# An inverse put behind the next row maximum, and a second scale factor of ones, in a two-layer attention trunk

## The reference

```python
for l in range(DEPTH):                       # DEPTH 2, 512 tokens, 1024 channels
    h = rms_norm(x, norm_g[l])
    proj = jnp.einsum('btd,dc->btc', h, w_in[l])
    q_a, kv_a, g_a, z_a, q_b, k_b, v_b, f_b, z_b, merge = jnp.split(proj, split_at, axis=-1)
    y_a = nsa_mixer(q_a, kv_a, g_a, ...) * jax.nn.silu(z_a)
    y_b = fox_mixer(q_b, k_b, v_b, f_b, b_forget[l]) * jax.nn.silu(z_b)
    ...
# NSA: three softmaxes per head, each output times its own gate
    o = g[:, :, 0] * o_cmp + g[:, :, 1] * o_slc + g[:, :, 2] * o_win
# FOX: one softmax per head, no gate on the probabilities
    s = s + Fq[..., None] - F[:, :, None, :]
    p = masked_softmax(s, mask)
    return jnp.einsum('bhqk,bkhd->bqhd', p.astype(v.dtype), v)
```

## Time and profile before

| | us |
|---|---|
| median of 3 runs | 1521.31 |
| lowest, highest | 1521.21, 1521.73 |
| the profiled execution | 1520.49 |
| its span, first to last instruction | 1518.8 |
| PE busy | 1477.1 (97%) |
| DVE busy | 1028.8 (68%) |
| ACT busy | 903.8 (60%) |
| POOL busy | 488.2 (32%) |
| granted TensorE clock, mean | 0.994 of full |

### The profile page before, as it was taken

The page is one execution under the profiler, slowest core; times in us unless marked ns, Lnnn a source line. Parts: engine busy times, 40 slices in busy tenths (PEclk is TensorE's granted clock), DMA queues, the critical chain, the costliest instruction groups (busy, mean ns, idle before and its releaser), DMA issues.

```text
span 1518.8 us, 24823 instructions
## 1 busy us (share of the span) xinstructions
PE 1477.1 (97%) x7605; PEld 1242.0 (82%) x7605; DVE 1028.8 (68%) x2459; ACT 903.8 (60%) x1879; POOL 488.2 (32%) x578
## 2 busy tenths in 40 slices
PE   6999999999999999999998999999999999999997
PEld 5778888888888888888876888888888888888886
DVE  4778788788788874434557778788787787643443
ACT  4667777777777762223446777777777776422233
POOL 1245445455455320000004445355355363000000
PEclk9999999999999999999999999999999999999998
DMA  9222222122122243332452222222222221433332
GB/s 245 70 72 56 57 52 60 47 53 62 49 56 56 57 123 99 89 105 83 126 152 67 60 53 57 55 56 57 56 57 55 55 56 45 149 88 106 89 95 80
DMA packets 221826, 117.84 MB, mean 78 GB/s; under 512 B 17560, under 2 KB 220336, under 8 KB 221232
## 3 DMA queue, kind: packets, MB, share of 16 engines
q1 hardware_dynamic: 219584, 107.66, 26.8%
q0 software_dynamic: 1728, 8.66, 1.5%
q10 hardware_dynamic: 432, 0.54, 0.1%
HBM read 110.41 MB, written 6.42 MB: 77 GB/s over the span
## 4 chain that ended last, share of the span: by engine, by line
PE 84%; DVE 6%; ACT 3%; SPq 2%; issue 2%; DMA 2%; POOL 1%; ACTq 0%; DVEq 0%; POOLq 0%
PE acc L1522 59%; PE o_pair L1600 8%; PE turned L1582 7%; PE scores L1573 4%; PE scores L1574 4%; DMA w_raw<-in_w_in_dram 2%; DVE w_lo L1031 1%; PE misc L1611 1%; SPq L462 1%; DVE c_blk L1310 1%; ACT w_hi L700 1%; SPq L469 1%; DVE yt_lo L1408 1%; PE o_pair L1626 0%; PE turned L1680 0%
## 5 line engine op out<-in xcount | busy, mean ns | idle before, releaser
L1522 PE MATMUL acc<-u_hi,w_hi 128*128 128x512 f32 x1120 | 443.1, 396 | 9.4 <-DVE w_lo L1031 5.8
L1522 PE MATMUL acc<-u_lo,w_hi 128*128 128x512 f32 x1120 | 441.1, 394 | 0.0
L1522 PE MATMUL acc<-u_hi,w_lo 128*128 128x512 f32 x1120 | 440.2, 393 | 0.0
L816 ACT ACTIVATE prob<-prob,row_max 128x128 f32<-128x128 f32 (+3 forms) x384 | 215.3, 561 | 183.4 <-DVE row_max L1197 181.2
L1031 DVE TENSOR_TENSOR w_lo<-w_raw,w_hi 128x1024 fp32r<-128x1024 f32 x188 | 233.8, 1244 | 87.9 <-ACT w_hi L700 85.3
L628 POOL TENSOR_SCALAR prob<-prob,row_inv,gates 128x128 f32<-128x128 f32 (+3 forms) x256 | 173.0, 676 | 331.1 <-DVE row_inv L1204 329.5
L700 ACT ACTIVATE w_hi<-w_raw 128x1024 fp32r<-128x1024 f32 x188 | 198.1, 1054 | 95.4 <-PE acc L1522 85.8
L1522 PEld LDWEIGHTS acc<-u_hi,w_hi 128*128 128x128 f32 x1120 | 211.0, 188 | 51.9 <-DVE w_lo L1031 7.6
L1522 PEld LDWEIGHTS acc<-u_hi,w_lo 128*128 128x128 f32 x1120 | 211.0, 188 | 40.0
L1522 PEld LDWEIGHTS acc<-u_lo,w_hi 128*128 128x128 f32 x1120 | 211.2, 189 | 38.7
L1197 DVE CUSTOM_DVE_ANT_0 prob<-scores,causal 128x128 f32<-128x128 f32 (+3 forms) x384 | 184.9, 481 | 46.4 <-PE scores L1574 37.5
(11 more groups left out here) (195 smaller groups left out, 2235.0 us busy)
## 6 DMA issues: line engine op xcount, KB each, us to landing
w_raw<-in_w_in_dram SPq DMA_DIRECT2D x140, 512.0 KB, 3.8
w_raw<-in_w_proj_nsa_dram SPq DMA_DIRECT2D x16, 512.0 KB, 3.7
w_raw<-in_w_proj_fox_dram SPq DMA_DIRECT2D x16, 512.0 KB, 3.7
w_raw<-in_w_out_dram SPq DMA_DIRECT2D x16, 512.0 KB, 3.7
x_scratch<-xT POOLq DMA_DIRECT2D x2, 2048.0 KB, 9.0
xT<-x_scratch POOLq DMA_DIRECT2D x2, 2048.0 KB, 8.3
x_nat<-in_x_dram SPq DMA_DIRECT2D x4, 512.0 KB, 6.5
c_w<-in_cmp_w_k_dram SPq DMA_DIRECT2D x4, 512.0 KB, 7.8
```

Source lines behind the costliest of these rows:

```text
L816: act.activation(prob[:, ring, 0:width], prob[:, ring, 0:width], ACT.Exp, bias=row_max[:, ring:ring + 1], scale=-1.0, accum_out=row_sum[:, ...
L1522: ins = pe.matmul(acc[par][0:width, :], w[:, par, k, 0:width], rhs, start=(n == 0), stop=(n == 23))
```

## The change

Two edits. In VectorE's stream the maximum of step s now stands ahead of the inverse of step s-1, where it stood behind it. And FOX's scaling gets a second factor per row, the first column of `ones`, so that it has the same form as NSA's.

```diff
@@ scale_step
                 if branch is None:
-                    ins = pool.tensor_scalar(p, p, row_inv[:, ring:ring + 1], None, ALU.mult)
+                    ins = pool.tensor_scalar(p, p, row_inv[:, ring:ring + 1], ones[:, 0:1], ALU.mult, ALU.mult)
@@ VectorE, body of a cycle
+                    if step(0):
+                        max_step(*step(0))
                     if step(LAG_SCALE):
                         invert_step(*step(LAG_SCALE))
-                    if step(0):
-                        max_step(*step(0))
                     if step(LAG_PT):
                         lo_step(*step(LAG_PT))
```

## The result

The changed kernel takes 1528.42 us (median of 5 runs, 1528.10 to 1528.99) where the kernel before takes 1521.21 (5 runs, 1520.81 to 1521.73). The ratio is 1.0048, interval 1.0033 to 1.0063: slower by 7.2 us, and outside of the forecast range. The profiled execution took 1528.11, its span is 1526.4 against 1518.8.

The account below looks back on a forecast made before the run. TensorE was taken as the bound. Per layer +0.20 - 0.70 = -0.50, two layers -1.0, middle cycles 0.0: 1519.5 against the profiled 1520.49, and 1520.3 us as median, range 1519.0 to 1523.5.

Parts of the forecast that it names:

- What bounds the kernel: TensorE, busy throughout the middle cycles; time can be gained only at its six waits in the two layers' last cycles.
- the faster rival: Softmax chain sets the pace: all six TensorE waits go, 3.6 us gained, 1517.7; chance of over 0.2% faster 3%.
- The cost of a late tile: At a transpose on TensorE: a late scaled tile costs its lateness plus 0.11 us; margins under 0.11 begin to cost.
- Part 1, middle cycles, step 7: New order delays the inverse 0.20 us; step 7's margin falls from 0.34 to 0.14, above 0.11, so no cost.
- Part 1, middle cycles, step 13: Inverse later by at most the maximum's 0.53 us; step 13's margin falls from 0.67 to 0.14, so no cost.
- the upper bound of 2.8 us: Middle cycles: delay of 0.35 us costs 1.4 us at step 7, with as much again from steps 11 and 13.
- The second rival: Inverse too late in every middle cycle, at step 7: 1521.7, or 1523.1 with steps 11 and 13; chance 22%, 5% beyond 0.2%.
- Part 2, step 22 of the last cycle: Faster FOX scalings on GpSimd remove TensorE's wait at step 22: -0.70 us per layer, range 0 to -0.70.
- Part 1, last cycle: Step 7's margin is used up, so +0.20 us per layer, 0 to 0.35; the wait for a low part unchanged.
- Part 2, the two-factor form's times: FOX scalings on GpSimd take 0.77, 0.66 and about 0.55 us for 512, 384 and 256 keys.
- The rival that the factor brings no speed: FOX's scalings stay slow for another reason than form: 1522.8 to 1524.2; chance 8%, 2% of it beyond 0.2%.

Follow-up runs that it names:

- late7: qcos_late plus one useless 256-column PSUM copy on VectorE between step 8's maximum and step 7's inverse in the 12 middle cycles; 1523.72 us.
- order_only: Kernel before with only the new order, maximum ahead of inverse; FOX's scaling keeps one factor; 1534.49 us, ratio 1.0083.
- qcos_psum: Changed kernel, but VectorE's cosine product in the cycles reads its first input from a PSUM bank, giving wrong values; 1520.81 us, ratio 0.9996.
- qcos_late: Changed kernel with VectorE's cosine product of the query rotation one slot later, nothing left out; 1520.48 us, ratio 0.9995.
- old_collide: Kernel before, old order and one factor, with the cosine product called ahead of the low part in its slot; 1528.01 us, ratio 1.0039.
- ones_only: Kernel before with only FOX's second factor of ones, old order kept; 1521.43 us, ratio 0.9998.

## Why the prediction was wrong

- **What bounds the kernel**: right. TensorE had no wait in the middle, so nothing could be gained there. The exponential's wait for maxima shrank from 181.2 to 177.3 us and brought nothing; the faster rival was rightly at 3%.
- **The cost of a late tile** (lateness plus 0.11): right, by late7 (0.25 worked out, 0.24 to 0.27 measured) and by step 13 (0.49 late and 0.60 worked out, 0.6 to 0.75 measured). At step 22 of order_only it gives 0.21 where 0.20 to 0.30 is lost.
- **Part 1, middle cycles, step 7: no cost**: right. The delay was forecast at 0.20 and took 0.34 - 0.20 = 0.14 off the margin.
- **Part 1, middle cycles, step 13: no cost**: this is the step that failed. "0.67 - 0.53 = 0.14, no cost" moved the scaling by its delay and let it keep its 0.55. The delay itself was sized safely: 0.27 and not 0.53, so that 0.41 of margin is left without the collision, as qcos_psum shows. What it left out is that a moved instruction gets new neighbours, and that its duration can depend on them. Fourteen scalings came to lie beside the cosine product and took 0.89 us more. Neither the sum nor the upper bound of 2.8 us nor a rival held such a term. It was to be had: the grouped view of the kernel before shows a shape that takes longer than one of twice its size,

```profile
L628 POOL TENSOR_SCALAR prob<-prob,row_inv,gates 128x128 f32<-128x128 f32 x64 | 45.0, 704 | 5.9 <-DVE row_inv L1204 4.3
...
L628 POOL TENSOR_SCALAR prob<-prob,row_inv,gates 128x256 f32<-128x256 f32 x64 | 36.4, 569 | 154.4 <-DVE row_inv L1204 154.4
```

since 14 of the 16 scalings of step 0 take 1.47 us beside VectorE's work, as do step 4's in the first cycle of each layer (1.49), and the others 0.45. FOX's 384-key scalings take 1.25 at step 18 and 1.68 to 1.76 at step 22; the 1.69 stands in the earlier trace rows, and the prediction read it as the form's price.
- **The second rival** (a late inverse in every middle cycle) had the sign and the kind of place: a tile of an NSA step too late for its transpose, twelve times, though it named step 7 ahead of 13, and step 7 cost nothing. Its price was put at 1.4 to 2.8 us and its mechanism, a delay, was another. Its condition, a delay of 0.57, was met in effect by 0.27 of delay and 0.89 of stretch, against the margin of 0.67.
- **Part 2, step 22 of the last cycle: -0.70**: the mechanism was right and the size off. The scaling was taken at 0.66, and took 1.10 beside a product of line 1145 with two SBUF inputs (itself 1.16 long where the kernel before has 0.67 to 0.70: GpSimd's gating ran when it started). The wait shrank to 0.27 us, not to nothing. The timeline there, changed kernel (the GpSimd row groups steps 22 and 23, 1.10 and 0.77 long with hardly a gap):

```profile
543.70 1.16 DVE L1145 SCALAR_TENSOR_TENSOR z_silu<-z_th,z_silu 128x512 f32<-128x512 f32 x1
...
544.29 1.85 POOL L625 TENSOR_SCALAR prob<-prob,row_inv,ones 128x384 f32<-128x384 f32 x2
...
545.12 0.28 PE L1600 MATMUL o_pair<-pt_lo,v_fox 128*128 128x256 f32 x1
...
545.45 0.55 PE L1582 MATMUL turned<-ident,prob 128*128 128x128 f32 x3
```

- **Part 1, last cycle: +0.20 at step 7, the low part's wait unchanged**: wrong in both places. Step 7's wait moved to step 6, whose scaling lies beside the query's low parts (line 1116), and step 13 gained one. Before, the last cycle lost 0.61, 0.59 and 0.70 us at step 7, at the low part and at step 22. After, it loses 0.70, 0.77 and 0.27 at steps 6, 13 and 22: 1.74 against 1.90, where 0.50 less was forecast. Step 6:

```profile
508.69 1.39 DVE L1116 TENSOR_TENSOR q_fox<-qk_raw,q_fox 64x512 fp32r<-64x512 f32 x2 [0.21 <-ACT q_fox L748]
508.75 1.71 POOL L628 TENSOR_SCALAR prob<-prob,row_inv,gates 128x384 f32<-128x384 f32 x1
...
510.51 0.55 PE L1582 MATMUL turned<-ident,prob 128*128 128x128 f32 x3 [0.48 <-POOL prob L628]
```

- **Part 2, the two-factor form's times**: right. FOX scalings of 512 keys have a mean of 766 ns after, against 1563. The rival that the factor brings no speed fell.

```profile
L625 POOL TENSOR_SCALAR prob<-prob,row_inv,ones 128x512 f32<-128x512 f32 x32 | 24.5, 766 | 17.0 <-DVE row_inv L1204 17.0
```

Without the collision the sum came out nearly as forecast: 1520.48 and 1520.81 for the two kernels that avoid it, against 1520.3. They are the changed kernel less one overlap, and stand in for it. That they come so near is in part luck: the last cycles give 0.16 and 0.18 in qcos_late's trace where 1.0 was forecast for the two, and the cycles ahead of them, put at 0.0, are together 0.35 shorter than before.

## What to carry to other kernels

When an edit moves an instruction of VectorE or GpSimd, list what it will lie beside, not only how much later it is; where one reads two SBUF tiles on VectorE and the other reads SBUF on GpSimd, let the loser end at the other's end plus up to its own duration, and compare that with the margin. A form whose instances have two durations, or a mean above that of a larger shape, is the sign of such a pair in the trace of the kernel before. And an engine made faster off the critical path can win a port from an instruction that is on it.

## What the runs showed of the hardware

**VectorE and GpSimd hold each other up** when the first reads two SBUF tiles and the second reads SBUF. The pairs seen: a 256-key scaling 0.55 alone, 1.44 beside the cosine product; a 384-key scaling 0.66 alone, and 1.16, 1.10 and 1.71 beside others; the query's sum 1.29 first and 2.25 second; the weight block 1.23 first and 2.33 second. With one of VectorE's inputs in PSUM there is no effect (0.56). The Trainium skill, page "SBUF — State Buffer", section "Who interferes with whom", states this: the second input of such a VectorE instruction comes through the shared read interface, which is GpSimd's only one, and the page calls the shared pair an exclusive lock. The trace agrees that the two are in each other's way. The loser ends behind the winner by less than its own full time (0.43 of 0.55 at step 13, 1.15 of 1.29 for the sum, 1.08 of 1.23 for the weight block), so these rows don't show that it stands still from its recorded start. The page read against the moved instructions would have put the missing term on the prediction's list.

**Who waits can't be read from the recorded starts.** The same section says that the issue order decides who blocks. The weight block wins with a start recorded 0.13 us ahead of the sum, and loses with one recorded 0.04 behind. But step 13's scaling is recorded 0.34 us ahead of the cosine product, and is still the one that is stretched, its end 0.43 behind the product's. In old_collide it is 0.21 ahead and is stretched to 1.33. In ones_only a scaling recorded 0.24 ahead of the product of line 1145 keeps 0.67, and that product takes 0.97. At which moment GpSimd takes the port these runs don't settle, nor whether a stretched scaling does a part of its work first.

**On GpSimd one factor is slower than two.** At 512, 384, 256 and 128 columns undisturbed one-factor scalings take 1.57, 1.25, 0.93 and 0.61 us and two-factor ones 0.77, 0.66, 0.55 and 0.45. The cause isn't settled; only the two forms were compared, at the same places in the program.
